# Two hybrid transformer layers on one core: token ranges of the projection strips cut to 516 tokens, their two halves re-cut at 256, and the places of the split weights in SBUF

## The reference, cut to what matters

```python
# layer 1, the convolution branch
conv = cb * short_conv(cc * cx, conv_w)              # 3 taps, causal, over positions
...
# layer 2
o = o * jax.nn.silu(g_r[:, :L])
gates = jax.nn.sigmoid(merge[:, :L])
mix = (gate_sb * (sb @ w_sb_out[l]) + gate_gla * (o @ w_gla_out[l])) @ w_o[l]
h = h + _rmsnorm(mix, norm_mix_post[l])
hn = _rmsnorm(h, norm_ffn_pre[l])
up = hn @ w_ffn_up[l]
act = jax.nn.gelu(_causal_dwconv(up, conv_w[l], conv_b[l]), approximate=True)   # 3 taps
ffn = (act * (hn @ w_ffn_gate[l])) @ w_ffn_down[l]
return h[:, N_META:]
```

## Time and profile before

| | us |
|---|---|
| median of 3 runs | 2101.61 (2101.34 to 2101.74) |
| the profiled execution | 2101.67 |
| its span in the profile | 2099.9 |
| TensorE (PE) busy | 2086.3 (99%) |
| weight loads (PEld) busy | 1850.4 (88%) |
| VectorE (DVE) busy | 1243.7 (59%) |
| ScalarE (ACT) busy | 831.4 (40%) |

### The profile page before, as it was taken

How to read it: one execution, slowest core, us unless ns; L and a number is a source line. 1 busy time by engine, 2 the same in 40 slices (tenths; PEclk the granted TensorE clock), 3 DMA queues, 4 the chain that set the end, 5 groups by cost and what they waited for, 6 DMA issues and landing times.

```text
span 2099.9 us, 33880 instructions
## 1 busy us (share of the span) xinstructions
PE 2086.3 (99%) x13662; PEld 1850.4 (88%) x13662; DVE 1243.7 (59%) x1847; ACT 831.4 (40%) x1305; POOL 164.6 (8%) x146
## 2 busy tenths in 40 slices
PE   9999999999999999999999999999999999999998
PEld 8998988898888788899898888999999998889897
DVE  7775444565555555777664666367855567546364
ACT  4333222433444443434434566343424344222233
POOL 0012000030000000232120000022300000000000
PEclk9999999999999999999999999999999999999999
DMA  4343222522222233332323221231133222332323
GB/s 151 111 168 113 86 76 61 199 83 83 72 69 71 96 106 98 109 111 81 110 91 100 81 92 59 83 122 58 55 137 108 91 80 89 94 98 90 101 91 100
DMA packets 53563, 203.36 MB, mean 97 GB/s; under 512 B 6960, under 2 KB 7344, under 8 KB 52288
## 3 DMA queue, kind: packets, MB, share of 16 engines
q1 hardware_dynamic: 49248, 177.56, 26.3%
q10 hardware_dynamic: 3232, 20.80, 2.5%
q0 software_dynamic: 960, 3.24, 0.5%
HBM read 190.96 MB, written 10.62 MB: 96 GB/s over the span
## 4 chain that ended last, share of the span: by engine, by line
PE 93%; DVE 4%; ACT 2%; issue 0%; DMA 0%; SPq 0%; DVEq 0%; ACTq 0%
PE ps L2176 69%; PE ps L2299 7%; PE ps L2775 5%; PE ps L2641 1%; PE ps L2423 1%; PE ps L2448 1%; PE ps L2376 1%; PE ps L2707 1%; PE ps L2547 1%; DVE kk_r L1829 1%; PE ps L2462 1%; ACT kk L966 1%; ACT kk L967 1%; PE ps L2685 0%; PE ps L2528 0%; PE ps L2355 0%
## 5 line engine op out<-in xcount | busy, mean ns | idle before, releaser
L556 ACT ACTIVATE wh<-wraw 128x1024 fp32r<-128x1024 f32 x284 | 300.3, 1057 | 738.8 <-PE ps L2176 625.0
L1236 DVE TENSOR_TENSOR wl<-wraw,wh 128x1024 fp32r<-128x1024 f32 x298 | 366.1, 1230 | 128.0 <-ACT wh L556 124.4
L2176 PE MATMUL ps<-xh,wh 128*128 128x264 f32 (+1 forms) x1800 | 325.3, 325 | 0.6 <-DVE tmp L1269 0.5
L2176 PE MATMUL ps<-xl,wh 128*128 128x264 f32 (+1 forms) x1800 | 317.2, 321 | 0.0
L2176 PE MATMUL ps<-xh,wl 128*128 128x264 f32 (+1 forms) x1800 | 316.8, 320 | 0.0
L2176 PEld LDWEIGHTS ps<-xh,wh 128*128 128x128 f32 x1800 | 264.4, 188 | 30.1 <-issue 2.4
L2176 PEld LDWEIGHTS ps<-xl,wh 128*128 128x128 f32 x1800 | 265.2, 188 | 25.7
L2176 PEld LDWEIGHTS ps<-xh,wl 128*128 128x128 f32 x1800 | 265.2, 188 | 25.2
L2176 PE MATMUL ps<-bh,wh 128*128 128x264 f32 (+1 forms) x1296 | 231.7, 322 | 0.3 <-ACT wh L556 0.2
L2176 PE MATMUL ps<-bl,wh 128*128 128x264 f32 (+1 forms) x1296 | 227.8, 319 | 0.0
L2176 PE MATMUL ps<-bh,wl 128*128 128x264 f32 (+1 forms) x1296 | 227.8, 319 | 0.0
(11 more groups left out here) (533 smaller groups left out, 2775.3 us busy)
## 6 DMA issues: line engine op xcount, KB each, us to landing
wraw<-weights_dram SPq DMA_DIRECT2D x299, 512.0 KB, 3.5
qq<-weights_dram SPq DMA_DIRECT2D x12, 512.0 KB, 4.6
kk<-weights_dram SPq DMA_DIRECT2D x12, 512.0 KB, 4.5
hf<-tables_dram POOLq DMA_DIRECT2D x12, 264.0 KB, 3.0
res<-x_t_dram SPq DMA_DIRECT2D x4, 528.0 KB, 7.2
res<-x_t_dram ACTq DMA_DIRECT2D x1, 2112.0 KB, 8.9
res_dram<-res ACTq DMA_DIRECT2D x1, 2112.0 KB, 6.4
mrg_dram<-mrg ACTq DMA_DIRECT2D x1, 2112.0 KB, 8.7
```

Of the source, the lines that this page charges most:

```text
L556: nc.scalar.activation(wh[:, slot], wraw[:, slot], ACT.Copy).then_inc(hi_done, 1)
L1236: nc.vector.tensor_tensor(wl[:, slot], wraw[:, slot], wh[:, slot].bitcast(F32), ALU.subtract)\
L2176: last = nc.tensor.matmul(o, w[:, slot, c, :], a[:, c, tok], start=(k == 0), stop=(k == len(steps) - 1))
```

## The change

It has four parts.

1. Strips whose meta tokens feed only a convolution, or nothing that is kept, run on 516 tokens, 12 to 527 (`USED` = 516): the two gate strips out of three of the first layer's convolution (16 strips), in the second layer the merge gates of the stick-breaking branch (8), its output projection (4), the GLA output gate (8), the GLA merge gates (8), the GLA output projection (8), `w_o` (8), and the up strips of the FFN (22). These are 82 strips. The elementwise work on their rows is cut to the same tokens.
2. A strip of n tokens is split as 256 columns and the rest: 256 and 260 for the 516 (tokens 12 to 267 and 268 to 527), 256 and 272 for the 57 strips that keep all 528 tokens. The first piece goes to columns 256 to 511 of its bank, so that the two pieces are contiguous in PSUM.
3. `wh` and `wl` get a pad of 16 numbers per slot (slots 4160 bytes apart in place of 4096), and the weights of a 516-token strip are written 12 numbers, 48 bytes, further into the slot. The strips of the second FFN's down projection are placed 48 bytes further too.
4. Loops that split strips for the next phase have their last turn written out, since its place may differ; the save and reload of `mrg` in DRAM moves 516 of 528 tokens.

```diff
+SPLIT = SEQ // 2
+USED = T - 12
...
+WIDTH = [SEQ] * NSTRIP
+for _name in ("ret_qkv", "diff_qkv", "sb_main", "gla_lr", "gla_main"):
+    WIDTH[START[_name]:START[_name] + dict(PHASES)[_name]] = [T] * dict(PHASES)[_name]
+for _name, _first in (("sb_main", 12), ("sb_proj", 0), ("gla_main", 16), ("gla_gates", 0), ("gla_proj", 0), ("w_o", 0)):
+    for _n in range(_first, dict(PHASES)[_name]):
+        WIDTH[START[_name] + _n] = USED
+for _n in range(24):
+    WIDTH[START["conv_in"] + _n] = SEQ if _n % 3 == 2 else USED
+for _g, _n in enumerate(FFN2_GROUPS):
+    WIDTH[START[f"glu{_g}up"]:START[f"glu{_g}down"]] = [USED, SEQ] * _n
+PLACE = [T - USED if w == USED else 0 for w in WIDTH]
+for _g in range(len(FFN2_GROUPS)):
+    PLACE[START[f"glu{_g}down"]] = T - USED
...
+def strip_at(w, n, slot):
+
+    o = PLACE[n if isinstance(n, int) else slot.first]
+    return w[:, int(slot), o:o + KC * P].rearrange("p (k n) -> p k n", k=KC)
...
-        wh, wl = sb("wh", [P, 2, KC, P], F32R), sb("wl", [P, 2, KC, P], F32R)
+        wh, wl = (sb(n, [P, 2, KC * P + NM], F32R) for n in ("wh", "wl"))
...
+        def wide_at(b, n):
+
+            return ps[:, b:b + 2, :].rearrange("p b n -> p (b n)")[:, SPLIT:SPLIT + n]
+
+        def pieces(b, n):
+
+            if n == SEQ:
+                return [(slice(NM, T), ps[:, b, :])]
+            middle = T - n + SPLIT
+            return [(slice(T - n, middle), ps[:, b, SPLIT:2 * SPLIT]), (slice(middle, T), ps[:, b + 1, 0:n - SPLIT])]
...
-                nc.scalar.activation(wh[:, slot], wraw[:, slot], ACT.Copy).then_inc(hi_done, 1)
+                nc.scalar.activation(strip_at(wh, n, slot), wraw[:, slot], ACT.Copy).then_inc(hi_done, 1)
...
-                with act.Fori(0, count // 2) as i:
+                with act.Fori(0, count // 2 - 1) as i:
                     for j in range(2):
                         split_hi(*pos(B, j + 1, i))
+                for k in (count - 1, count):
+                    split_hi(*pos(B, k))
...
-            act.dma_start(mrg_dram, mrg[:]).then_inc(mrg_saved, 16)
+            act.dma_start(row_all(mrg_dram), row_all(mrg)).then_inc(mrg_saved, 16)
...
-                rows = [(slice(NM, T), ps[:, bank, :])] if n == SEQ else \
-                    [(slice(HALF * k, HALF * k + HALF), ps[:, bank + k, 0:HALF]) for k in range(2)]
+                rows = pieces(bank, n)
...
                     for tok, o in rows:
-                        last = nc.tensor.matmul(o, w[:, slot, c, :], a[:, c, tok], start=(k == 0),
+                        last = nc.tensor.matmul(o, strip_at(w, number, slot)[:, c, :], a[:, c, tok], start=(k == 0),
                                                 stop=(k == len(steps) - 1))
```

More of the change, by code:

```diff
@@ L2184, in glu_sums @@
                 for q in range(2):
-                    last = nc.tensor.matmul(ps[:, 4 + q, 0:HALF], ones, qq[:, 0, HALF * q:HALF * q + HALF], start=True,
+                    first = T - USED + USED // 2 * q
+                    last = nc.tensor.matmul(ps[:, 4 + q, 0:USED // 2], ones, qq[:, 0, first:first + USED // 2], start=True,
                                             stop=True)
@@ L2195, in product @@
                 def product(p, c, w, a):
-                    for k in range(2 if p is up else 1):
-                        o, tok = (ps[:, 2 * p[2] + k, 0:HALF], slice(HALF * k, HALF * k + HALF)) if p is up else \
-                            (ps[:, 2 * p[2], :], slice(NM, T))
-                        ins = nc.tensor.matmul(o, w[:, p[2], c, :], a[:, c, tok], start=(c == 0 and w is wh and a is xh),
+                    for tok, o in pieces(2 * p[2], USED if p is up else SEQ):
+                        ins = nc.tensor.matmul(o, strip_at(w, p[0], p[2])[:, c, :], a[:, c, tok],
+                                               start=(c == 0 and w is wh and a is xh),
                                                stop=(c == KC - 1 and a is xl))
@@ L2250, in first_strip @@
                     for w, a in ((wh, xh), (wh, xl), (wl, xh)):
-                        for k in range(2):
-                            last = nc.tensor.matmul(ps[:, k, 0:HALF], w[:, 0, c, :], a[:, c, HALF * k:HALF * k + HALF],
+                        for tok, o in pieces(0, USED):
+                            last = nc.tensor.matmul(o, strip_at(w, 0, 0)[:, c, :], a[:, c, tok],
                                                     start=(c == 0 and w is wh and a is xh),
@@ L2583, in strip_by_halves @@
                 pe.wait_ge(hi_done, n + 1)
-                for k in range(2):
+                for k, (tok, o) in enumerate(pieces(0, WIDTH[n])):
                     pe.wait_ge(*waits[k])
@@ L2589, in strip_by_halves @@
                         for c in range(KC):
[L2590 to L2591 removed]
+                            last = nc.tensor.matmul(o, strip_at(w, n, slot)[:, c, :], a[:, c, tok],
+                                                    start=(w is wh and a is bh and c == 0),
                                                     stop=(w is wl and c == KC - 1))
@@ L2639, in _ @@
                         for c in range(4):
-                            for k in range(2):
-                                last = nc.tensor.matmul(ps[:, z + k, 0:HALF], w[:, slot, 4 * o + c, :],
-                                                        a[:, c, HALF * k:HALF * k + HALF],
+                            for tok, dst in pieces(z, USED):
+                                last = nc.tensor.matmul(dst, strip_at(w, n, slot)[:, 4 * o + c, :], a[:, c, tok],
                                                         start=(w is wh and a is xh and c == 0), stop=(w is wl and c == 3))
```

171 lines of the change are left out of this document (94 added, 77 removed).

## The result

The changed kernel takes 2114.66 us (median of 4 runs, 2114.41 to 2114.74) against 2101.68 of the kernel before beside it: 13.0 us more, ratio 1.0062, interval 1.0049 to 1.0074. It was forecast at 2099.2, with 2108 as the upper end, so the prediction was wrong, in sign and in range.

A forecast was written before the change was run, and what follows sets the result against it. The prediction took the time to be TensorE's matmuls at their spacing. Its terms, -5.1 + 2.1 - 1.4 + 4.8 - 3.0 + 0.2 + 0, sum to -2.4 us, giving 2099.2 us, range 2090 to 2108.

The forecast's parts named there:

- The bound: Whole kernel: TensorE busy 99% of the span, time a sum of matmuls at their start-to-start spacing, other engines counting only if late.
- "Alike" and "unlike": Matmul operands both at a multiple of 128 bytes or both 64 behind, 120.0 ns for 256 columns; otherwise 113.5 or 117.8.
- Item 5: 512-column matmuls in weight slot 1 become unlike and gain: -3.0 us, between 0 and -8.7.
- Item 7: Down projection, 528 matmuls whose moving weights start 48 bytes further while tokens don't: 0, ends +-3.4 us.
- Items 1 to 4: Pairs of 516 tokens in slots 0 and 1: -5.1 and +2.1 us; pairs of 528: -1.4 and +4.8.
- Item 6: Products of line 2299 in slot 1: 228 become alike, 192 unlike, +-4.4 ns each, +0.2 us.
- At no cost: Shifted weight writes, unrolled last turns, evictions and `mrg` DMAs stay covered and add no wait: no time.
- Columns alone: Rival, whole kernel: places in SBUF matter little, so 23,616 columns saved give 9.8 us, 2091.8; chance 0.28.
- The slower rival: Slot 1 becomes alike through the pad's 64 bytes, unlike strips cost 117.8 ns, 512 columns gain nothing: +6.6, 2108.2; chance 0.20.
- Steps: Rival: matmul costs come in steps of 6.67 ns, so 260 columns pay for 272; 2102.6, no change; chance 0.12.

## Why the prediction was wrong, point by point

- *The bound.* Right: the time is the sum of the matmuls' spacings. All 13 us are found in them; no wait of TensorE has grown by more than 0.2 us in all.
- *"Alike" and "unlike" within 128 bytes.* This is the step beneath the failure. Rows 8 did show that place matters, and the runs bear that out: two kernels with the same instructions are 22.9 us apart by addresses. The Trainium skill ("TensorE: Matmul & The Clock Gate", part 2) gives the array two independent SBUF read ports; what the prediction drew from that, that the places of the two operands can't matter, is not borne out here. Whether the ports themselves are the reason no run shows. But the modulus is 256: 128 bytes more, which leave "alike" alike, cost 32.5 us. By 128 I took slot 0 for untouched; in truth only its high part kept its distance.
- *Item 5, 512 columns in slot 1, -3.0 us, ends 0 and -8.7.* This is the term that failed. It came out as **+12.7**. I carried the gain of 256 columns over to 512, and left out a loss, though the only long ones at another distance took 620 ns where my price for alike ones was 607, so they pointed at a loss. At distance 192 they cost 5.9 ns more than at 0. Slot 1's share is 7.7 of the 12.7 us (1344 matmuls); slot 0's `wl` pass, now at distance 128, lost 3.9, and its two passes that stayed at distance 0 lost 1.1.
- *Item 7, down projection, 0 with +-3.4.* +2.2, within its ends, but for another reason. The diff sets the place of only the first strip of each of the three groups, not of all as the text ahead of the prediction says. The loss comes almost all from the slots' places, and the pad alone gives it too (+2.3).
- *Items 1 to 4, the strips in two pieces, +0.4 together.* -1.8, close to the forecast by luck, since the items are off in both directions. A 516-token pair cost 236.3 ns in slot 0 (232.9 forecast) and 237.8 in slot 1 (241.7), a 528-token pair 241.6 (237.9) and 245.3 (246.7). Against 240.3 before, that is about -2.9, -3.1, +0.9 and +3.6 us where -5.1, +2.1, -1.4 and +4.8 were forecast: two of the four have the other sign.
- *Item 6, +0.2.* +0.4. *At no cost.* Right: waits, evictions, the `mrg` DMAs show nothing.
- *Columns alone, 2091.8.* Not borne out for the changed kernel, and its reason, that places matter little, is refuted. Its number is that of the kernel with the pad of 64, 2091.80, where the cut pairs cost 235.2 ns in place of 240.3, 5.1 against the 5.0 of twelve columns.
- *The slower rival, 2108.2.* The right place, the 64 bytes of slot 1, and the right sign, but with the wrong price: the pairs came to -1.8 us where it held +6.5, and the 512-column strips, for which it held nothing, lost all of it.
- *Steps, 2102.6.* Not borne out: a piece of 260 cost 118.9 ns at the distance (192) at which 272 cost 124.3.

## What to carry to other kernels

When a pad or a new tile is put before or between operands of TensorE in a kernel like this one (fp32r, 128x128 weight blocks; other types were not measured), list the addresses of moving and stationary operands modulo 256 before and after, for every slot and every part, also for the matmuls that the change doesn't mean to touch. Choose pads that are whole multiples of 256 bytes (64 bytes a slot cost 22.9 us in the kernel before, 256 bytes nothing), and shift an operand only inside such a frame. And when a cost is bounded from a row at another size, keep a loss within the bounds unless something excludes it.

## What the runs showed of the hardware that I had not expected

- For fp32r matmuls of 128x128 stationary weights the spacing changes with the places of the two operands in a partition, and a distance modulo 256 bytes orders what was measured: 512 columns 227.4 ns at 0, 229.9 at 64, 232.6 at 128, 233.3 at 192, 233.2 at 224. A step of 32 bytes counts; one of 256 does not.
- Which operand is ahead counts: with the roles changed over, in the down projection, distance 64 costs 229.0 ns and 192 costs 233.3, while 32 costs 233.3.
- The best distance depends on the size: 0 for 512 columns, while two pieces of 264 are equally well off at 0 and at 192 (240.5 and 240.3 ns) and 5 ns worse at 128. A first piece of 256 cost 114.4 ns at 160 and 115.9 at 192, its second piece of 272 cost 125.9 and 124.3.
- When the distance changes between strips, the map of the uniform kernels doesn't hold exactly: 229.0 ns on average at distance 0 in the changed kernel against 227.4 before, and 232.5 at 64 against 229.9. Why the places matter in this way stays open; the runs show the map, not its cause.
